# The second half of w_out is issued behind the x of token tiles 12 and 13

## What is computed

```
h    = RMSNorm_pre_mix(x) * (1 + scale1) + shift1
[v_pool | x_conv | B | C] = h @ w_in
y_A  = pool_scale * groupwise_linear(mean_window(v_pool) - v_pool)     windows 2/4/8/16
y_B  = B * dwconv3_causal(C * x_conv)
x    = x + gate1 * RMSNorm_post_mix([y_A | y_B] @ w_out)
h2   = RMSNorm_pre_ffn(x) * (1 + scale2) + shift2
u    = dwconv3_causal(h2 @ ffn_w_up);  [a | b] = u
x    = x + gate2 * RMSNorm_post_ffn((silu(a) * b) @ ffn_w_down)
```

## Time and profile before

| | |
|---|---|
| median of 3 runs | 750.41 us (749.32 to 774.93) |
| the profiled execution | 750.26 us; span of its slowest core (core 1) 748.7 us |
| spans of the 8 cores | 745.6 to 748.7 us |
| granted TensorE clock, mean | 0.986 to 0.992 |
| PE busy | 688.7 us (92%) |
| VectorE, ScalarE, POOL busy | 481.8 (64%), 343.0 (46%), 235.0 us (31%) |
| DMA, POOL queue (q0) | 54.19 MB, 42.3% of the 16 engines' span |
| DMA, SP queue (q1) | 42.47 MB, 17.1% |

### The profile page before, as it was taken

The page is one execution under the profiler, slowest core; times in us unless marked ns, Lnnn a source line. Parts: engine busy times, 40 slices in busy tenths (PEclk is TensorE's granted clock), DMA queues, the critical chain, the costliest instruction groups (busy, mean ns, idle before and its releaser), DMA issues.

```text
span 748.7 us, 11934 instructions; the slowest of 8 cores (745.6 to 748.7 us)
## 1 busy us (share of the span) xinstructions
PE 688.7 (92%) x4020; PEld 331.0 (44%) x4020; DVE 481.8 (64%) x640; ACT 343.0 (46%) x605; POOL 235.0 (31%) x268
## 2 busy tenths in 40 slices
PE   0179996999999999999999999999999999999996
PEld 0144553454544444444444444444444444444443
DVE  0258865789887886786877422258888888833222
ACT  1326644573748797683554411134545454521111
POOL 4102210001004644433554300006676667540000
PEclk9989999999999999999999999999999999999999
DMA  8999998469442897699898333325443443013311
GB/s 145 215 186 242 223 211 152 118 142 217 151 158 79 181 220 177 141 168 198 135 173 144 57 112 113 113 88 111 73 69 61 82 83 60 1 41 141 113 65 48
DMA packets 30488, 97.42 MB, mean 130 GB/s; under 512 B 4480, under 2 KB 4864, under 8 KB 30300
## 3 DMA queue, kind: packets, MB, share of 16 engines
q0 software_dynamic: 17024, 54.19, 42.3%
q1 hardware_dynamic: 13404, 42.47, 17.1%
HBM read 125.28 MB, written 19.07 MB: 193 GB/s over the span
## 4 chain that ended last, share of the span: by engine, by line
PE 74%; DMA 13%; DVE 4%; ACT 3%; issue 3%; POOL 2%; SPq 0%; DVEq 0%; ACTq 0%; POOLq 0%
PE ps L810 45%; PE ps L298 22%; PE ps L289 7%; DMA arena<-w_in_p 5%; DMA arena<-x 4%; DMA arena<-st_ffn 2%; ACT arena L561 1%; DMA scr<-arena 1%; PE ps L306 1%; ACT arena L729 1%; POOL arena L955 1%; DVE arena L1183 1%; POOL arena L542 1%; POOL arena L1197 0%; DVE arena L606 0%
## 5 line engine op out<-in xcount | busy, mean ns | idle before, releaser
L810 PE MATMUL ps<-arena 128*128 128x512 bf16 (+1 forms) x2400 | 437.9, 343 | 13.9 <-ACT arena L845 6.3
L810 PEld LDWEIGHTS ps<-arena 128*128 128x128 bf16 x2400 | 200.8, 98 | 240.8 <-issue 22.3
L298 PE MATMUL ps<-arena 128*128 128x512 bf16 (+1 forms) x748 | 161.9, 379 | 0.0
L1183 DVE SCALAR_TENSOR_TENSOR arena<-ps,arena 128x1023 f32<-128x1023 f32 x88 | 112.6, 1279 | 42.8 <-ACT arena L1181 42.5
L1197 POOL TENSOR_TENSOR arena<-arena 128x1024 bf16<-128x1024 f32 x44 | 103.7, 2356 | 82.2 <-DVE arena L1187 46.2
L1187 DVE SCALAR_TENSOR_TENSOR arena<-ps,arena 128x1022 f32<-128x1022 f32 x88 | 112.8, 1281 | 9.2
L298 PEld LDWEIGHTS ps<-arena 128*128 128x128 bf16 (+1 forms) x748 | 73.7, 99 | 87.9 <-issue 0.4
L568 DVE RECIPROCAL arena<-arena 128x1 f32<-128x1 f32 (+1 forms) x67 | 10.7, 159 | 137.1 <-ACT arena L563 136.4
L1181 ACT ACTIVATE arena<-ps,arena 128x1024 f32<-128x1024 f32 x88 | 97.6, 1110 | 0.1
L561 ACT ACTIVATE arena<-ps 128x1024 f32<-128x1024 f32 (+1 forms) x33 | 33.7, 1022 | 137.6 <-PE ps L298 119.6
L289 PE MATMUL ps<-arena 128*128 128x512 bf16 (+2 forms) x344 | 72.4, 359 | 0.8 <-DVE arena L568 0.7
(11 more groups left out here) (88 smaller groups left out, 405.4 us busy)
## 6 DMA issues: line engine op xcount, KB each, us to landing
arena<-w_up POOLq DMA_DIRECT2D x44, 512.0 KB, 7.3
y<-arena SPq DMA_DIRECT2D x32, 512.0 KB, 2.7
arena<-w_ada POOLq DMA_DIRECT2D x24, 512.0 KB, 17.0
arena<-x SPq DMA_DIRECT2D x22, 512.0 KB, 8.7
arena<-y SPq DMA_DIRECT2D x16, 512.0 KB, 3.8
arena<-w_down POOLq DMA_DIRECT2D x11, 512.0 KB, 13.1
arena<-x POOLq DMA_DIRECT2D x10, 512.0 KB, 29.6
arena<-w_in_j POOLq DMA_DIRECT2D x4, 768.0 KB, 39.8
```

The source lines that it names most:

```text
L298: inst = e.matmul(out_ap, lhs_list[i], rhs_list[i], start=(first and i == 0), stop=(last and i == n - 1))
L810: inst = e.matmul(o_, l_, r_, start=st, stop=sp_)
L1183: K.op("dve", lambda e: e.scalar_tensor_tensor(tv[:, 1:1024], psv[:, 0:1023], fw_of(1, c), tv[:, 1:1024], ALU.mult, ALU.add), reads=rp + [ ...
```

## The change

`wout_load` takes a list of halves. At n = 2 only the first half is issued; the second is issued at n = 6, right behind the x loads of tiles 12 and 13.

```diff
-    def wout_load():
-        for hb in range(2):
+    def wout_load(hbs=(0, 1)):
+        for hb in hbs:
...
-            wout_load()
+            wout_load((0,))
         if n == 6:
             for t in (12, 13):
                 h_load(t, "pool")
+            wout_load((1,))
```

## The result

The changed kernel took 771.0 us in the median of 6 runs (770.3 to 772.0; two more executions took 777.2 and 781.3), the kernel before 750.1 us beside it: a ratio of 1.029, 95% interval 1.027 to 1.032. The forecast was 749.6 us and no change. The time came out above the whole range, and the kernel slower where no change was forecast.

A forecast was written before the change was run, and what follows sets the result against it. PE, busy 92% of the span, was taken as the bound; its waits near 112 to 122 us would fall from 6.35 to 5.7 us, so 750.26 - 0.65 = 749.6 us, range 747.2 to 752.3, no change.

The forecast's parts named there:

- Point 1: POOL queue: without the second w_out half ahead, x of tiles 12 and 13 lands 6.4 us earlier.
- lower bound (1.4): x of tile 13 lands 1.4 us behind tile 12 instead of 2.5, giving 748.6 us.
- Rival C: POOL queue: x moves up by less than forecast, so the kernel takes 752.2 to 753.4 us; chance 0.13.
- Point 2: The w_out half moved back lands about 115 us, first read at 141.5: cost nothing, 26 us of cover.
- Points 3 and 4: ScalarE's squares delay L845 of P(6) by 7.5 us to 110.0; PE waits 1.4 us, L914 comes at 115.6.
- Point 5: Gate piece 3 waits 4.2 us for VectorE L776; two paths end together, P(8) starts at 118.0 instead of 118.25.
- Point 6: Sum on core 1: PE's waits fall from 6.35 to 5.7 us, a gain of 0.65 us.
- The clock's 1.3 us stay: PE at P(8): the low-clock cost of 1.3 us remains, since PE still stands for 4.2 us.
- The 0.02 for slower: Whole kernel: chance of measuring slower than before, given to the unknown.
- Rival B: PE around P(8): with the wait split, the clock stays up and saves 1.3 us more, 748.3 us; chance 0.12.
- Rival A: PE ahead of P(8): the 5.94 us wait and 1.3 us of clock vanish, 743.0 us; chance 0.10.
- Rival D: Operations of n = 8 to 11 that changed places cost or give something, 748.5 to 751.5 us; chance 0.13 beyond forecast's bounds.

The follow-up runs named there:

- gate early: Changed kernel with only VectorE's L776 of gate piece 1 moved up directly behind its L775: 747.4 us, ratio 0.998.
- Queue alone: Kernel before, only the second w_out half moved behind x of tile 13 on the POOL queue: 745.2 us (0.995), another session 743.4 us (0.992).
- both back: Changed kernel with ScalarE's squares and roots of tiles 12 to 14 behind L913, VectorE's L568 of tile 12 behind L914 of V(6): 746.85 us, 0.996.

## Why the prediction was wrong, point by point

**Point 1, the queue: right, undersized.** The jump was put at 6.4 us with x at 106.3 and 108.8; it landed at 105.1 and 106.5. The first half itself landed 1.7 us sooner than before (103.3 for 105.0), and x of tile 13 came 1.4 us behind tile 12 instead of 2.5; this gap was the prediction's own lower bound (1.4). Rival C, and the 2.4 us that the Trainium skill (DMA: Bandwidth & Descriptors, Anatomy of one DMA) would give, are refuted: the second half, now last, landed 6.6 us behind x of tile 13.

**Point 2: right.** The half that moved back landed at 113.1, and `O_mm` starts at 138.69 without a wait for it.

**Points 3 and 4: right in kind, 2.3 us too late.** L845 of P(6) ran at 107.66, not 110.0, and L914 of V(6) at 113.26, not 115.6. V(6) still covers PE at 107.66, so the forecast wait of 1.4 us ahead of P(7) is not there. Had the bound of 1.4 been taken between the two landings, 1.0 of the 2.3 would have been foreseen; the earlier first half is the rest.

**Point 5: right.** The wait of 4.2 us for L776 was 3.24 on core 1 (2.3 to 4.0 on the others) and the tie of both paths is confirmed by gate early. P(8) gained 2.1 us instead of 0.25.

**Point 6, the sum: here it failed.** On core 1 the gain was 2.8 us at `O_mm` against the forecast 0.65. That flatters: on the mean `O_mm` starts at 140.6 us on the eight cores of before and at 139.1 on the six undisturbed ones, 1.5 us sooner. Over the slowest cores, in the four later sessions, the changed kernel stands at 0.998 to 0.999, 1.1 to 1.5 us under the kernel before: better than forecast by 0.5 to 0.9 us, and at 747.6 to 748.2 inside the range. The intervals of these ratios are 0.2 to 0.3% wide, so that such a gain can be told from nothing, which the prediction denied with its 2%. The sentences that broke are "The clock's 1.3 us stay" and "Behind this the work per engine is the same, PE waits hardly anywhere, so the shift is kept". They price the clock only over P(8), and take the clock behind it for granted. The traces of before hold no stretch at 0.81 in their rows and so no price for it; the one sign was that an execution of before had taken 774.9 us. With 24 us, the term left out was nearly forty times the gain that was summed up. The 0.02 for slower had no mechanism behind it, and Rival B asked only whether the clock would stay up, not what a new order right behind its return might do.

**Rival A** was right as physics and wrong for this kernel: with ScalarE's order of before the wait does vanish and the kernel goes to 0.992 to 0.995, 743.4 to 745.2 us, against its 743.0. The scheduler's reordering, a side effect of its model of the load, took 3 to 4 us of that back. Queue alone beats both kernels clearly, both back the changed one by 0.8 us, with intervals that overlap; neither had a pair at 0.81. **Rival D** is not seen: from the start of `O_mm` to the end the undisturbed cores take 605.8 to 605.9 us, and those of before 605.8 to 606.1, but for core 1 with 607.2, of which 1.3 is one wait for VectorE L1187 that no other core had.

## What to carry to other kernels

Moving a load moves two things where a scheduler models it, the data and everyone's order; run each alone by fixing the lists, since the gain here (-0.5 to -0.8%) sat in the first and was mostly given back by the second. On a metric of the slowest core look at each core's span and clock before any wait: six of eight cores said faster, and the verdict came from two. A change that leaves a pause of PE but alters what follows it should be timed in more than one session: the same kernel had a pair in 8 of 8 executions and in 3 of 40. Removing the pause by the queue alone gave 3.9 and 5.7 us; that it also keeps the low state away is not shown.

## What the runs showed of the hardware that was not expected

- Pairs of cores (0 and 1, 2 and 3, 4 and 5, 6 and 7) were granted 0.81 of TensorE's clock from 5 to 8 us after the clock had come back from 0.5, both cores starting together to 0.5 us, for 159 to 161 us, and the span grew by about 24 us. It ended at 285 to 287 us of the span (four pairs); whether its length or the place in the program ends it was not tried.
- The Trainium skill (TensorE: Matmul & The Clock Gate, the note on the peak-current limiter) has this level of 13/16, but for a whole die once three of its cores run dense matmuls, and for as long as the load lasts. Here eight cores ran them at 1.00 for nearly the whole span, core 1 with 157.9 us of PE in 162 among them, and only pairs fell. The measurement decides: the rule doesn't describe this kernel's normal state.
- A pause of 2.3 us could leave the clock at 1.0 (core 3 of the profiled execution, with 0.6 us more behind P(8)), where 3.2 us did not: P(8) took 1.9 us there and 3.0 on core 1. But its length alone didn't decide: in the third session's changed kernel core 6 fell to 0.5 at 114.9 us behind a pause of 1.85 us (P(8) took 3.27 us), and in the fourth's core 5 stayed at 1.0 behind 2.52 us (1.89).
- A w_out half held the queue for 6.6 us also when it was last, against 6.4 before the change, though only 1 MB of it is written; two x tiles with 1 MB together took 3.8 us.
